# Scan layer of a two-block kernel: decays on ScalarE alone, triangle taken ahead of the gates, last squares by ScalarE

## The reference, cut to what matters

```python
def step(state, inp):
    x_c, a_c, b_c, c_c = inp
    acs = jnp.cumsum(a_c, axis=1)
    seg = acs[:, :, None] - acs[:, None, :]
    decay = jnp.exp(jnp.where(causal, seg, -jnp.inf))
    cb = jnp.einsum("blgn,bsgn->blsg", c_c, b_c)
    y_diag = jnp.einsum("blsgr,bsgrp->blgrp", cb[..., None] * decay, x_c)
    y_off = jnp.einsum("blgn,bgrpn->blgrp", c_c, state) * jnp.exp(acs)[..., None]
    ...

def gated_group_rms_norm(y, z, g):
    u = y * silu(z)
    u = u.reshape(shp[:-1] + (SSM_GROUPS, SSM_D_INNER // SSM_GROUPS))
    u = u * lax.rsqrt(jnp.mean(u * u, axis=-1, keepdims=True) + EPS_2)
    return u.reshape(shp) * g
```

## Time and profile before

| what | value |
|---|---|
| median of three runs | 2035.9 us |
| profiled execution, its own time | 2034.78 us |
| its span, first to last instruction | 2033.0 us |
| mean granted TensorE clock | 0.996 |
| TensorE busy (matmuls) | 1966.4 us, 97% |
| VectorE busy | 1381.4 us, 68% |
| ScalarE busy | 865.5 us, 43% |
| GpSimd busy | 253.9 us, 12% |

### The profile page before, as it was taken

The page is one execution under the profiler, slowest core; times in us unless marked ns, Lnnn a source line. Parts: engine busy times, 40 slices in busy tenths (PEclk is TensorE's granted clock), DMA queues, the critical chain, the costliest instruction groups (busy, mean ns, idle before and its releaser), DMA issues.

```text
span 2033.0 us, 24999 instructions
## 1 busy us (share of the span) xinstructions
PE 1966.4 (97%) x9434; PEld 1559.6 (77%) x9434; DVE 1381.4 (68%) x2046; ACT 865.5 (43%) x1342; POOL 253.9 (12%) x231
## 2 busy tenths in 40 slices
PE   7999999999999999999999999898999998999997
PEld 5787888888888776788888887687777776876665
DVE  7996476546645449657635654988888888437986
ACT  4574243222233348643222323444443444236773
POOL 3040100000010000010000001233333332000002
PEclk9999999999999999999999999999999999999999
DMA  7455323232233220032233223221222213322012
GB/s 225 109 140 151 100 85 105 81 114 94 85 103 105 92 85 10 5 107 86 84 108 107 93 78 94 83 63 52 78 84 73 80 61 101 96 82 72 28 32 78
DMA packets 79623, 178.33 MB, mean 88 GB/s; under 512 B 17680, under 2 KB 31248, under 8 KB 79504
## 3 DMA queue, kind: packets, MB, share of 16 engines
q1 hardware_dynamic: 75792, 169.92, 27.2%
q0 software_dynamic: 3424, 6.23, 1.2%
q10 hardware_dynamic: 288, 0.59, 0.1%
HBM read 169.43 MB, written 7.27 MB: 87 GB/s over the span
## 4 chain that ended last, share of the span: by engine, by line
PE 70%; DVE 18%; ACT 5%; issue 5%; DMA 1%; SPq 0%; POOL 0%; DVEq 0%; POOLq 0%; ACTq 0%
PE psum L430 16%; PE psum L433 16%; PE psum L431 16%; DVE wl L401 2%; PE psum L471 2%; PE psum L474 2%; PE psum L472 2%; PE psum L855 1%; PE psum L857 1%; PE psum L856 1%; ACT wh L390 1%; PE psum L452 1%; DVE mE L1654 1%; PE psum L455 1%; DVE mE L1673 1%
## 5 line engine op out<-in xcount | busy, mean ns | idle before, releaser
L401 DVE TENSOR_TENSOR wl<-raw,wh 128x1024 fp32r<-128x1024 f32 (+3 forms) x337 | 391.9, 1165 | 326.9 <-ACT wh L390 326.4
L430 PE MATMUL psum<-xh,wh 128*128 128x512 f32 x1368 | 541.6, 396 | 1.3 <-DVE mbc L1531 0.9
L433 PE MATMUL psum<-xh,wl 128*128 128x512 f32 x1368 | 533.7, 390 | 1.3 <-DVE wl L401 1.3
L431 PE MATMUL psum<-xl,wh 128*128 128x512 f32 x1368 | 532.9, 390 | 0.0
L390 ACT ACTIVATE wh<-raw 128x1024 fp32r<-128x1024 f32 (+3 forms) x337 | 315.5, 938 | 272.9 <-PE psum L433 168.5
L430 PEld LDWEIGHTS psum<-xh,wh 128*128 128x128 f32 x1368 | 257.0, 188 | 61.5 <-DVE mbc L1531 3.4
L433 PEld LDWEIGHTS psum<-xh,wl 128*128 128x128 f32 x1368 | 256.8, 188 | 56.7 <-DVE wl L401 2.9
L431 PEld LDWEIGHTS psum<-xl,wh 128*128 128x128 f32 x1368 | 257.0, 188 | 55.1 <-issue 2.6
L578 POOL TENSOR_TENSOR rs<-rs,sq 128x512 f32<-128x512 f32 x41 | 54.2, 1322 | 1087.8 <-ACT sq L563 1087.6
L431 PE MATMUL psum<-fl,wh 128*128 128x512 f32 x352 | 137.0, 389 | 0.0
L433 PE MATMUL psum<-fh,wl 128*128 128x512 f32 x352 | 137.0, 389 | 0.0
(11 more groups left out here) (500 smaller groups left out, 3355.4 us busy)
## 6 DMA issues: line engine op xcount, KB each, us to landing
raw<-d_w SPq DMA_DIRECT2D x224, 512.0 KB, 3.5
raw<-d_w SPq DMA_DIRECT2D x32, 384.0 KB, 3.1
raw<-d_w SPq DMA_DIRECT2D x48, 256.0 KB, 2.6
raw<-d_w SPq DMA_DIRECT2D x32, 320.0 KB, 2.9
Mt<-d_kd SPq DMA_DIRECT2D x64, 64.0 KB, 2.4
bc<-d_bc SPq DMA_DIRECT2D x8, 256.0 KB, 3.3
d_ud<-ust SPq DMA_DIRECT2D x8, 256.0 KB, 3.2
U<-d_ud POOLq DMA_DIRECT2D x64, 32.0 KB, 2.9
```

The source lines that it names most:

```text
L401: dve.e.tensor_tensor(K.wl[n % NH][:, 0:COLS[n]], K.raw[n % RAW][:, 0:COLS[n]], K.wh[n % NH][:, 0:COLS[n]].bitcast(F32), ALU.subtract).the ...
L430: pe.e.matmul(b[:, :], WH[:, o:o + P], XH, start=(k == k0), stop=False)
L431: pe.e.matmul(b[:, :], WH[:, o:o + P], XL, start=False, stop=False)
L433: mm = pe.e.matmul(b[:, :], WL[:, o:o + P], XH, start=False, stop=(k == k1 - 1))
```

## The change

In the decay step VectorE no longer takes part. ScalarE computes, block by block, Relu(own sum - spread) with the own sum as a bias per partition (now positive, from the `upper` constant), and the exponential after it is taken with scale -1. Above the diagonal this gives 1 in place of 0; so the triangle is applied to the product of B and C instead: VectorE multiplies it with the constant `upper` while it takes it out of PSUM (`cb_dve`), where ScalarE copied it before. That multiplication stands, in VectorE's order, at the last `convend` of a group, ahead of `z`, and in the first group at the first `turn`. The semaphore `mlow` goes and `mcm` comes; ScalarE's `mcb` counts only its remaining copies. For the last group, ScalarE squares both halves, each square waits for the second cast of the scaling of group 6 (`muh` 14), GpSimd has no part in it, and TensorE sums the two with two accumulating matmuls.

```diff
@@ seg_pe
-    for n, (con, j) in enumerate([("nupper", j) for j in range(4)] + [("slower", j) for j in range(3)]
+    for n, (con, j) in enumerate([("upper", j) for j in range(4)] + [("slower", j) for j in range(3)]
@@ cb_pe
-    take(pe, bank, ("mcb", 3 * g + 1))
+    take(pe, bank, ("mcm", g + 1))
...
-    take(pe, bank, ("mcb", 3 * g + 2))
+    take(pe, bank, ("mcb", 2 * g + 1))
@@ cb_act
-    act.wait_ge("mEm", 4 * g)
-    act.wait_ge("mcbp", 3 * g + 1)
-    act.e.activation(K.mcb[:, :, :], K.bank[MB[("cb", g, 0, 0)]][:, :].rearrange("p (n c) -> p n c", c=P),
-                     ACT.Copy).then_inc(K.S["mcb"], 1)
     act.wait_ge("mcbp", 3 * g + 2)
...
+def cb_dve(K, dve, g):
+    dve.wait_ge("mEm", 4 * g)
+    dve.wait_ge("mcbp", 3 * g + 1)
+    dve.e.tensor_tensor(K.mcb[:, :, :], K.bank[MB[("cb", g, 0, 0)]][:, :].rearrange("p (n c) -> p n c", c=P),
+                        K.con("upper").unsqueeze(1).broadcast_to([P, 4, P]), ALU.mult).then_inc(K.S["mcm"], 1)
-def decay_dve(K, dve, hd):
...
 def decay_act(K, act, hd):
-    act.wait_ge("mlow", hd + 1)
+    act.wait_ge("msp", hd + 1)
+    act.wait_ge("msd", hd // 2 - 1)
     act.exp()
+    for j in range(4):
+        out = act.e.activation(E[:, j, :], R[:, j, :], ACT.Relu, scale=-1.0, bias=K.mbias[:, j, hd:hd + 1])
+    out.then_inc(K.S["act"], act.up())
     act.e.activation(E[:, 4:7, :], R[:, 1:4, :], ACT.Exp).then_inc(K.S["mdx"], 1)
-    act.e.activation(E[:, 0:4, :], E[:, 0:4, :], ACT.Exp).then_inc(K.S["mex"], 1)
+    act.wait_ge("act", act.n)
+    act.e.activation(E[:, 0:4, :], E[:, 0:4, :], ACT.Exp, scale=-1.0).then_inc(K.S["mex"], 1)
@@ weigh_dve
-    dve.wait_ge("mcb", 3 * g + 1)
+    dve.wait_ge("mcm", g + 1)
@@ scan_squares_act
+    if g == 7:
+        act.wait_ge("mu", 2 * g + 1)
+        act.wait_ge("muh", 2 * g)
+        act.e.activation(K.msq[:, :], K.mx[1][:, 0, :], ACT.Square).then_inc(K.S["msa"], 1)
     act.wait_ge("mu", 2 * g + 2)
@@ scan_sums_pe
-    pe.e.matmul(K.bank[bank][:, :], K.con("ones"), K.msq[:, :], start=True, stop=True).then_inc(K.S["mss"], 1)
+    mm = pe.e.matmul(K.bank[bank][:, :], K.con("ones"), K.msq[:, :], start=True, stop=(g < 7))
+    if g == 7:
+        pe.wait_ge("ms2", g + 1)
+        mm = pe.e.matmul(K.bank[bank][:, :], K.con("ones"), scan_square(K, g)[:, :], start=False, stop=True)
+    mm.then_inc(K.S["mss"], 1)
@@ mamba_dve
+        elif (what, g, i) == ("turn", 0, 0) or (what == "convend" and g and i == 3):
+            cb_dve(K, dve, g)
...
-        elif what == "decay":
-            decay_dve(K, dve, 4 * g + i)
@@ mamba_pool
-        elif what == "squares":
+        elif what == "squares" and g < 7:
```

More of the change, by code:

```diff
@@ L337 @@
     + ["mraw", "dtk", "mxs", "mset", "mseta", "msetp", "mci", "mcv", "mth", "mfin", "mz", "mzt", "mcbp", "mcb", "mtp", "mxt"]
-    + ["msp", "mlow", "mdx", "mex", "mEm", "mxe", "msd", "mup", "mu", "ms2", "msa", "mss", "mnv", "mny", "muh", "muo"]
+    + ["msp", "mcm", "mdx", "mex", "mEm", "mxe", "msd", "mup", "mu", "ms2", "msa", "mss", "mnv", "mny", "muh", "muo"]
     + ["lam", "lama", "akc", "aqc", "ag", "agg", "agt", "asp", "asc", "aex", "acm", "atp", "akp", "amix"]
@@ L1609, in states_pe @@
     pe.wait_ge("mxe", 2 * g + 1)
-    pe.wait_ge("mcb", 3 * g + 2)
+    pe.wait_ge("mcb", 2 * g + 1)
     for j in range(3):
@@ L1623, in states_dve @@
 def states_dve(K, dve, g):
-    dve.wait_ge("mcb", 3 * g + 3)
+    dve.wait_ge("mcb", 2 * g + 2)
     for j in (1, 2):
@@ L1723, in scan_squares_pool @@
     pool.wait_ge("mu", 2 * g + 1)
-    if g < 7:
-        pool.wait_ge("muh", 2 * g)
+    pool.wait_ge("muh", 2 * g)
     pool.e.tensor_tensor(K.msq[:, :], K.mx[g % 2][:, 0, :], K.mx[g % 2][:, 0, :], ALU.mult).then_inc(
```

## The result

| | before | after |
|---|---|---|
| median of the runs of this comparison | 2034.4 (5 runs) | 2026.2 (2021.97 to 2028.47, 5 runs) |
| ratio after to before | | 0.9943 [0.9931, 0.9954], some 11.6 us faster |
| profiled execution, its own time | 2034.78 | 2021.97 |
| its span | 2033.0 | 2020.0 |
| first to last B-C product (start to start) | 365.0 | 351.8 |

The forecast was 6.9 us faster, 2029, with a range from 2025. Taken plainly, the five times of each kernel lie 8.2 us apart in the median and 9.6 in the mean (2035.1 and 2025.4). The direction was right and the size too small.

A forecast was written before the change was run, and what follows sets the result against it. TensorE was taken as the bound, VectorE close behind. Removed waits 11.6 us less new waits 3.6 gave 8.0; less 1.35 in the tail, 6.65 off 2034.8: 2028.1, stated as 2029 for the median, range 2025 to 2035.

The forecast's parts named there:

- Everything in the earlier trace goes: Scan, 1320 to 1670: TensorE's listed idle waits, all hanging on VectorE, vanish when decay additions leave it; 11.6 us gained.
- the seven waits: Seven lines of TensorE idle time from 1320 to 1670: 5.7, 1.9, 1.1, 1.0, 0.9, 0.8 and 0.2 us.
- ScalarE takes VectorE's place: Scan decays: ScalarE's queue holds up convolution starts, five waits of 1.14 us stay; 0.95 us gained, 2035; 22 in 100.
- Relu needs table loads: ScalarE's decays: a table load each way, two per decay, 18 us in seven groups, 2047; 3 in 100.
- The term "11.6 us": Scan, 1320 to 1670: summed idle time VectorE makes TensorE spend, all taken as gained.
- New waits at the turn: TensorE waits for VectorE's masked B-C product: 0.6 us in four groups, 1.2 in another; 3.6 us lost.
- Steady part: Scan before the tail: 11.6 us of waits removed less 3.6 us of new ones, net 8.0 us gained.
- Tail: Last group: ScalarE's squares wait for `muh` 14, sums slow at the lower clock; 1.35 us lost, bounds 2.2 gained, 2.4 lost.
- Slower, at the turn: Masked product over 2.05 us late in five groups uses up the gain; with clock falls 9.5 us slower, 2045; 6 in 100.

The follow-up runs named there:

- the early multiplication: Changed kernel with VectorE's triangle multiplication moved to the step of the B-C product itself in groups 2 to 8; ratio to before 0.9931, steady part 349.4 us.
- the run again: The changed kernel measured and profiled once more, unaltered; ratio to before 0.9943, first to eighth B-C product 352.0 us, tail 40.5.
- the doubled Relus: Changed kernel with the four Relus of each decay made twice, the second four behind the end of the first; ratio to before 0.9983, steady part 360.4 us.

## Why the forecast was right in kind and too small in size

- **Everything in the earlier trace rows goes: right.** Not one of the seven waits is left between 1320 and 1670, with the decays alone or with the whole change. The rivals that ScalarE takes VectorE's place, or that Relu needs table loads, are out: Relus of 368 ns, four of them in 1.13 us (1.1 was taken, 1.27 was the other estimate), no load at them, periods of 52.7 without the triangle. The Trainium skill ("ScalarE: Activation LUTs", Table sets) had relu in every set, and the trace agrees: in the scan the same fifteen loads stand as before, at the logarithm and the gate. The rule of the Trainium skill (same page, Rules for kernel authors) to put relu on VectorE is not borne out for this place: a decay's four Relus hold ScalarE for 1.00 us up to its next start, as the additions held VectorE for 1.03, and ScalarE had the room. The reason that the rule gives is a speed in bf16, and these tiles are fp32.
- **What they are worth: this is the step that failed.** The term "11.6 us" was the sum of idle times as the waits view gives them. What went was 16.8 us (365.0 to 348.3 with the decays alone). That the whole change also came to 11.6 is chance. In periods 4 to 7 it is 8.7 us against 5.4 summed, 2.12 for each by the alignment: 0.27 more for each listed wait, and the two waits a group that the view leaves out. In the second and third period it is 7.6 against 6.15, and 0.5 in the first, where the clock fell in both executions.
- **New waits at the turn: right.** 3.6 us forecast; 351.8 - 348.3 = 3.5 measured: 0.8 in the third period for the wait of 0.96 (1.2 forecast), 0.6 in each of the next four (0.6 forecast), and 0.2 in the second for a wait that was put at nothing. The very first turn's 1.17 us was put at nothing too and did not show in its period (45.03 us against 45.04 without it, the latter with the clock down for a part). Here the price had been taken from starts (when the multiplication can end, when TensorE would start), not from an idle column, and it held. That the early multiplication takes 2.4 us of it away shows the place.
- **Steady part:** 8.0 forecast, 13.3 measured, all of the difference from the second point.
- **Tail: right, with the fall of the clock in another place in one execution.** The wait for `muh` 14 and its 2.1 to 2.2 us are shown by taking it away, the stretch by GpSimd by its absence. With the clock up the tail is 0.2 shorter than before (profile after), with the clock down 1.6 longer (the run again). Forecast were both, with the second as the likelier. Counted to the end of the span the two executions agree: 366.6 and 366.7 us from the last B-C product, against 365.1 before, so 1.5 and 1.6 us lost in either case, since the clock that was kept at the sums fell right behind the tail. Of the executions profiled with both squares on ScalarE and the wait, the changed kernel and the squares alone kept it at the sums, the changed one again, the early multiplication and the doubled Relus lost it.
- **Slower, at the turn:** out. The point was 2.05 us each, and the waits are 0.42 and once 0.96. Its "from 2.4 on the clock would also fall" was read from one row, and other rows do not bear it out (see the last section).

The sum with the term put right: -16.8 + 3.5 + 1.35 = -12, or -11.8 with the 1.5 us measured from the last B-C product on, and the ratio says -11.6. The interval was a second, smaller fault: its lower end took in every bound of the new waits and none of the removed ones, as if the record of idle time were exact.

What stays open is why whole times of one kernel spread by 5 to 7 us. They go with the mean granted clock (changed kernel: 2022.0 and 2023.4 at 0.997, 2026.2 to 2028.5 at 0.993 and 0.994), and traces show stretches at 0.50, in some executions only: some 3 us at 1304, some 3 to 7 around 1692, and 7 to 10 from 171 on; what decides on them was not tried. The clock is not all of it: the stretch ahead of the first B-C product, which no edit touches, took 1301.7 to 1305.3 us in the seven profiled executions without the fall at 171, and 1305.4 to 1308.3 in the five with it.

## What to carry to other kernels

When an engine is the bound at 97% and another runs late beside it, don't price the relief by the idle column of the waits view: it starts a wait only at the drawn end of a pipelined matmul, omits short ones, and leaves out the slower restart. Compare the starts of the same instructions with an undisturbed stretch of the same sequence; a group period does it in one number. And when an operation moves to another engine's list, look at what stands ahead of it there: the multiplication behind a split of weights cost four turns 0.6 us each, and a wait for a later step than needed cost 2.2. Last, read a short stretch together with the one behind it: a fall of the clock can lie in the one in one execution and in the other in the next (38.7 + 327.9 us and 40.5 + 326.3 here).

## What was not expected of the hardware

- The granted clock after an idle of TensorE is not a fixed answer: 3.53 us of idling left it at 2.4 GHz in one execution of the changed kernel, and 3.57 us in the same place brought it to 1.2 in another; 2.40 us did so in the kernel before. With the Relus twice, 2.13 us at a turn (1356.78) were followed by a fall and 3.18 us at the next (1403.92) were not. Where the clock falls matters too: at the sums of the kernel before VectorE's variance did not wait for it, and behind the tail it cost 1.6 us.
- Two waits on the same late engine don't add: 0.57 us put ahead of two short waits of the kernel before vanished in them, period 54.83 for 54.87.
- A VectorE pass with both operands in SBUF took 1.63 us beside a GpSimd pass and 0.69 without it, in the same place (1694.31 before, 1678.37 after); so in all twelve profiled executions, 1.63 in the four with GpSimd's squares and 0.69 in the eight without.
